# A hybrid decoder layer on one core: gate weights loaded once per group from GpSimd's queue, the low half of the recurrent y stored from another buffer, a split wait in the gate unit, and the chunk locals moved behind the head numerator

## The reference

```python
u = rmsnorm(h, pre_mix_gain)
proj = u @ w_in                      # rg_x, rg_gate, q, k, v, o (512 columns each), i, f (4 each)
# recurrent half (8 blocks of 64 channels)
xc = causal_conv4(rg_x)
r = sigmoid(xc @ gate_r_w + gate_r_b);  i = sigmoid(xc @ gate_i_w + gate_i_b)   # block diagonal
a = exp(-8 * r * softplus(-lam));  b = sqrt(1 - a*a) * (i * xc)
h_rg = scan(h = a*h + b);  y_rg = rmsnorm(h_rg * gelu(rg_gate))
# mLSTM half (4 heads of 128, chunkwise)
q, k = silu(causal_conv4(q)), silu(causal_conv4(k))
log_i, log_f = i + b_i, log_sigmoid(f + b_f)
# per chunk: cumulative log_f, running maxima, p = exp(d - m), scores = (q k^T) * p
# num = scores v + w * q C_prev ; state C carried from chunk to chunk
y_ml = headrmsnorm(sigmoid(o) * num / max(|den|, exp(-m)))
h = h + rmsnorm(concat(y_rg, y_ml) @ w_out)
h = h + rmsnorm(relu(rmsnorm(h) @ w_up)**2 @ w_down)
```

## Time and profile before

| | |
|---|---|
| median of 3 runs | 2432.08 us (2430.23 to 2432.1) |
| span of the profiled execution | 2429.1 us |
| TensorE busy | 2306.5 us, 95% of the span |
| VectorE busy | 1288.3 us, 53% |
| ScalarE busy | 659.1 us, 27% |
| GpSimd busy | 800.2 us, 33% |
| DMA, 16 engines | 244.82 MB, mean 101 GB/s |

### The profile page before, as it was taken

One profiled execution on the slowest core, in us unless ns is written; L12 is line 12 of the kernel. 1 busy time (PEld: TensorE's weight loads), 2 busy tenths in 40 slices (PEclk: granted clock), 3 DMA queues, 4 the chain that ended last, 5 costly groups with the idle time before them and its releaser, 6 DMA issues.

```text
span 2429.1 us, 29582 instructions
## 1 busy us (share of the span) xinstructions
PE 2306.5 (95%) x10549; PEld 1896.2 (78%) x10549; DVE 1288.3 (53%) x1665; ACT 659.1 (27%) x1187; POOL 800.2 (33%) x490
## 2 busy tenths in 40 slices
PE   5988899999996899999999999979899999999998
PEld 4766688888885687888888888868688888888886
DVE  4666556666656365534534543527745534534535
ACT  5554345445445231101100110124201101100112
POOL 6000000000000137534733743520845634733630
PEclk9999899999998899999999999989899999999999
DMA  5335454545432642111101211247311111211203
GB/s 192 115 132 201 150 163 148 189 131 181 159 113 70 220 144 79 52 35 52 60 28 50 69 35 37 101 141 249 120 44 61 52 34 52 69 35 35 69 17 147
DMA packets 123944, 244.82 MB, mean 101 GB/s; under 512 B 13040, under 2 KB 46160, under 8 KB 123888
## 3 DMA queue, kind: packets, MB, share of 16 engines
q1 hardware_dynamic: 95280, 141.20, 17.4%
q0 software_dynamic: 26304, 94.52, 12.3%
q10 hardware_dynamic: 2304, 8.39, 0.9%
HBM read 193.61 MB, written 50.46 MB: 100 GB/s over the span
## 4 chain that ended last, share of the span: by engine, by line
PE 61%; DVE 3%; ACT 1%; issue 1%; DMA 1%; POOL 0%; ACTq 0%; DVEq 0%; SPq 0%; PEldq 0%; POOLq 0%
PE o_ps L1373 20%; PE o_ps L1374 20%; PE o_ps L1375 20%; DVE o_relu L1649 1%; ACT o_ps L1474 1%; DVE o_ff_lo L1653 1%; PE o_ps L1397 0%; DMA o_v_lo<-ylo_d 0%; DVE o_acc L1593 0%; DVE o_v_lo L1642 0%; DMA o_w_raw<-in_w_out 0%; DVE o_h_t L1609 0%; ACT o_ff_hi L1531 0%; DVE o_h_t L1622 0%; POOL w_lo L1344 0%
## 5 line engine op out<-in xcount | busy, mean ns | idle before, releaser
L1342 POOL TENSOR_TENSOR w_hi<-o_w_raw,one 128x1024 fp32r<-128x1024 f32 x100 | 191.5, 1915 | 683.7 <-PE o_ps L1375 589.8
L1373 PE MATMUL o_ps<-o_v_hi,w_hi 128*128 128x512 f32 x1024 | 400.1, 391 | 4.8 <-DVE o_v_lo L1642 4.8
L1374 PE MATMUL o_ps<-o_v_lo,w_hi 128*128 128x512 f32 x1024 | 399.6, 390 | 0.0
L1375 PE MATMUL o_ps<-o_v_hi,w_lo 128*128 128x512 f32 x1024 | 399.6, 390 | 0.0
L1663 DVE TENSOR_TENSOR o_acc<-o_ps,o_acc 128x512 f32<-128x512 f32 x224 | 154.1, 690 | 377.1 <-PE o_ps L1375 376.6
L1649 DVE TENSOR_TENSOR o_relu<-o_relu 128x512 f32<-128x512 f32 x128 | 221.0, 1727 | 180.9 <-ACT o_relu L1528 180.3
L1528 ACT ACTIVATE o_relu<-o_ps 128x512 f32<-128x512 f32 x128 | 76.5, 598 | 872.1 <-PE o_ps L1375 842.9
L436 PE MATMUL m_unit_ps<-u_hi,w_hi 128*128 128x512 f32 x768 | 310.0, 404 | 0.0
L436 PE MATMUL m_unit_ps<-u_hi,w_lo 128*128 128x512 f32 x768 | 301.2, 392 | 0.0
L436 PE MATMUL m_unit_ps<-u_lo,w_hi 128*128 128x512 f32 x768 | 300.3, 391 | 0.0
L1653 DVE TENSOR_TENSOR o_ff_lo<-o_relu,o_ff_hi 128x512 fp32r<-128x512 f32 x128 | 243.6, 1903 | 90.7 <-ACT o_ff_hi L1531 90.7
(11 more groups left out here) (281 smaller groups left out, 3443.8 us busy)
## 6 DMA issues: line engine op xcount, KB each, us to landing
o_w_raw<-in_mlp_w_up POOLq DMA_DIRECT2D x64, 512.0 KB, 4.6
o_w_raw<-in_mlp_w_down POOLq DMA_DIRECT2D x64, 512.0 KB, 3.6
u_hi<-uhi_d SPq DMA_DIRECT2D x12, 2048.0 KB, 10.8
u_lo<-ulo_d SPq DMA_DIRECT2D x12, 2048.0 KB, 15.2
w_raw<-in_w_in POOLq DMA_DIRECT2D x24, 512.0 KB, 5.7
m_rows<-rows_d SPq DMA_DIRECT2D x16, 512.0 KB, 5.3
o_v_hi<-yhi_d SPq DMA_DIRECT2D x16, 512.0 KB, 5.5
o_v_lo<-ylo_d SPq DMA_DIRECT2D x16, 512.0 KB, 6.4
```

What stands on the lines that cost most here:

```text
L1342: pool.tensor_tensor(w_hi[i], w_raw[i % 2][:], one_bc, ALU.mult).then_inc(w_split[i], 1)
L1373: nc.tensor.matmul(dst, sh, mh, start=(i == 0), stop=False)
L1374: nc.tensor.matmul(dst, sh, ml, start=False, stop=False)
L1375: last = nc.tensor.matmul(dst, sl, mh, start=False, stop=(i == n - 1))
```

## The change

Five edits, all in `build_mixers`:

1. The gate weights of a group are loaded once, from GpSimd's queue (`load_gate_w`), instead of once a step from SP's. Group 0's four transfers stand between the loads of x tile 1 and `gate_rows(0)`; those of groups 1 to 3 behind the last raw weight of the group, with a wait for the last gate product of the group before. SP's `load_rows` no longer waits for `gate_mm`. TensorE waits for 64 more counts a group, not a step.
2. The low part of the recurrent y is written to `b_t` and stored from there. ScalarE's square of g_x waits only for VectorE's subtraction of the step before; the wait for the stores' landing moves to the square that writes `b_t`.
3. The gate unit waits for tiles 0 to 5 of u_lo, and in front of tile 6's matmuls for all eight.
4. `chunk_locals` moves on VectorE from behind `states` to behind `head_numerator`.
5. The semaphore `gate_w_in` is created outside the mixers' own set.

```diff
@@ load_rows (SP)
                 for n in ("iw", "s_old", "parg0", "kw_arg"):
                     sp.wait_ge(s[n], s.freed(p))
-                sp.wait_ge(s["gate_mm"], s.freed(p))
                 if isinstance(p, int) and p < NT:
                     sp.wait_ge(rows_out, 32 * (p + 1))
-                for r, name in enumerate(("rg_gate_r_w", "rg_gate_i_w")):
-                    for h in range(2):
-                        sp.dma_start(gate_w[64 * h:64 * h + 64, r, 64 * h:64 * h + 64],
-                                     a[name][0].rearrange("(g h) i j -> h i g j", h=2)[h, :, ds(p // NT, 1), :]
-                                     ).then_inc(gate_w_in, 16)
                 sp.dma_start(rows[:], k["rows_d"][:, ds(p * TILE, TILE)].partition_broadcast(P)
                              ).then_inc(rows_in, 16)
@@ store_rg (SP)
-                sp.dma_start(k["ylo_cols"][:, ds(m * TILE, TILE)], g_y[:].bitcast(F32)).then_inc(yrg_out, 16)
+                sp.dma_start(k["ylo_cols"][:, ds(m * TILE, TILE)], b_t[:]).then_inc(yrg_out, 16)
@@ GpSimd
+            def load_gate_w(g):
+                if not isinstance(g, int) or g:
+                    pool.wait_ge(s["gate_mm"], s.ready(g * NT - 1))
+                for r, name in enumerate(("rg_gate_r_w", "rg_gate_i_w")):
+                    for h in range(2):
+                        pool.dma_start(gate_w[64 * h:64 * h + 64, r, 64 * h:64 * h + 64],
+                                       a[name][0].rearrange("(g h) i j -> h i g j", h=2)[h, :, ds(g, 1), :]
+                                       ).then_inc(gate_w_in, 16)
-            for t in range(NT - 1):
+            load_x(1)
+            load_gate_w(0)
+            gate_rows(0)
+            for t in range(1, NT - 1):
                 load_x(t + 1)
                 gate_rows(t)
...
                     load_raw((c + 3) % 6, g + c // 3)
+                load_gate_w(g)
...
+            load_gate_w(NG - 1)
@@ gates_and_transposes, gate_unit (TensorE)
-                pe.wait_ge(gate_w_in, m * 64 + 64)
+                pe.wait_ge(gate_w_in, (m // NT) * 64 + 64)
...
-                pe.wait_ge(ulo_made, KT * (p + 1))
+                pe.wait_ge(ulo_made, KT * p + gap_tiles[5][0])
                 if p:
                     pe.wait_ge(prev_made, p)
                 for c in range(KT):
+                    if c == gap_tiles[5][0]:
+                        pe.wait_ge(ulo_made, KT * (p + 1))
@@ ScalarE: sigmoids_1, exponentials
-                act.wait_ge(yrg_out, m * 32 + 32)
+                freed("yrg_lo", m)
                 nc.scalar.activation(g_y[:], g_x[:], ACT.Square).then_inc(s["g2"], 1)
...
+                act.wait_ge(yrg_out, m * 32 + 32)
                 nc.scalar.activation(b_t[:], a_t[:], ACT.Square).then_inc(s["a2"], 1)
@@ VectorE: rg_low, period
-                nc.vector.tensor_tensor(g_y[:].bitcast(F32R), g_y[:], yrg_hi[:].bitcast(F32), ALU.subtract
+                freed("h", m + 1)
+                nc.vector.tensor_tensor(b_t[:].bitcast(F32R), g_y[:], yrg_hi[:].bitcast(F32), ALU.subtract
...
-                if gates:
-                    chunk_locals(p)
                 if mix:
                     recurrence(m)
                 low_of("k")
                 if mix:
                     head_numerator(m)
+                if gates:
+                    chunk_locals(p)
                 low_of("v")
```

More of the change, by code:

```diff
@@ L187, in build_mixers @@
         w_split = {u: sem("w_split_" + u) for u in UNITS}
-        gate_w_in = sem("gate_w_in")
+        gate_w_in = k["gate_w_in"]
         raw_first = k["raw_in_p"]
@@ L1759, in hybrid_layer @@
             "gates_in": ctx.enter_context(nc.semaphore("gates_in")),
+            "gate_w_in": ctx.enter_context(nc.semaphore("gate_w_in")),
         }
```

## The result

The change takes 2399.16 us (median of 4 runs, 2398.41 to 2401.31) where the kernel before takes 2432.09 (2430.23 to 2432.93) beside it: a ratio of 0.9873, 95% interval 0.986 to 0.9885, so 33 us or 1.3% faster. The forecast was 2401 us in a range of 2396 to 2410, with 31.6 us of gain in the span; the spans differ by 2429.1 - 2396.6 = 32.5.

What follows compares the result with a forecast made beforehand. TensorE, busy for 95% of the 2429.1 us span, bounds the kernel; gain is possible only where it waits. 14.8 + 5.4 + 8.95 + 9.7 less 7.3 gives 31.6 us: span 2397.5, forecast 2401 us, range 2396 to 2410.

Steps and rivals of the forecast that it cites:

- Edit 1, 14.8 us: At the gate products in periods 1 to 4, TensorE's waits for gate weights go: 14.8 us, nothing in their place.
- GpSimd's issues: Four issues ahead of gate_rows(0) in period 0 cost 0, at most 2.1 us; the skill's port rule would add 2.8.
- Edit 2, 0 us as cover: ScalarE's square stops waiting for DRAM, so its gate unit copy comes earlier; cover for the gate products, 0 us gain.
- Edit 3, 5.4 us: At the gate unit, TensorE's waits for the last low part of u go: 5.4 us.
- Edit 4, 8.95 us less 7.3: At the square sums, den2's waits go (8.95 us); new waits of 1.9, 1.9 and 3.5 us in periods 1 to 3.
- The clock, 9.7 us: TensorE's clock losses behind four removed waits in the early periods go: 1.7, 3.4, 1.7 and 2.9 us, together 9.7.
- no new loss: Behind the new TensorE waits of 0.7 to 2.1 us, no new clock loss was counted.
- if the clock still falls between 120 and 280 us: Sign that the prediction is wrong: TensorE's clock was to be 1.00 from period 1 to 300 us.
- rival A: The clock falls behind the new waits too, once in each of periods 1 to 3: 5.1 us, 2406; chance 0.18.
- B: Period 4's wait only changes name: TensorE waits 3.7 us for m_y_t plus 1.7 of clock, 2406; chance 0.07.
- C: No change: VectorE bounds the early periods throughout, and 27 of the 31.6 us return; chance 0.03.
- D: Slower: ScalarE stands for b_t's stores in every step from landings of 16.7 us; 2453 us at 21; chance 0.03.

Runs made afterwards that it cites:

- e7: The change with VectorE's convolution of x later and its split of q moved into an earlier pause: 2396.42 us (0.9856).
- e8: The change with GpSimd's four issues of gate weights behind gate_rows(0) instead of ahead of it: 2401.38 us (0.9876).
- e3: The change with the low y made in g_y again, ScalarE's square waiting until it has landed in DRAM: 2408.31 us (0.991).
- e2: The change with the gate unit waiting for all eight low parts of u again: 2406.65 us (0.9907).
- e5: The kernel before with only the chunk locals moved behind the head numerator: 2426.60 us (0.9984).
- e9: The change run once more, unaltered, beside another kernel on the same chip: 2399.24 us (0.9873).
- e1: The change with the chunk locals back ahead of the recurrence: 2406.51 us (0.9905).
- e4: The kernel before with only the gate weights loaded once per group, issued by GpSimd: 2411.52 us (0.9921).

## Why the prediction was right

**Edit 1, 14.8 us.** All four waits went, also the 9.22 us of period 4, with nothing in their place. The reason given holds in the trace. VectorE and, in the second row, ScalarE at the end of period 3:

```profile
239.05 0.73 DVE L992 SCALAR_TENSOR_TENSOR m_y_t<-m_s_ps,par,m_yml_hi 128x512 fp32r<-128x512 f32 x1
```

```profile
233.74 0.62 ACT L739 ACTIVATE m_yrg_hi<-m_g_y 128x512 fp32r<-128x512 f32 x1
```

m_y_t ends at 239.78, and TensorE is due at the transposes of o at 238.84 + 1.72 = 240.56. The margin is 0.8 us; the prediction had 1.1 (256.7 against 257.8). e7 used it up, and a wait of 0.85 us stood exactly there.

**GpSimd's issues.** All sixteen issues of gate weights, in ns min/median/max:

```profile
L345 POOL DMA_DIRECT2D m_gate_w<-in_rg_gate_r_w x8: 531/538/718, 42.5 to 568.5; - x8
L345 POOL DMA_DIRECT2D m_gate_w<-in_rg_gate_i_w x8: 522/529/562, 43.5 to 569.6; - x8
```

One of them took 0.18 us over the median, in the pair from 405.06 us, beside VectorE instructions of 0.55 us and more. e8, which takes the first four out of the way, is no faster. Of the rule of the Trainium skill ("SBUF — State Buffer", section "SBUF: two separate sides"), by which the prediction would have added 2.8 us, the four issues of period 0 say nothing. VectorE, the third value, did no work beside them:

```profile
42.48:44.57 2.09, 2.09 (x11) 1.70 (x11) 0.00 (x0) 0.00 (x0) 2.09 (x6) 1.00 0.90 310
```

So the 2.8 us could not come here, whatever the rule; the prediction's reason (the longest issue is 0.07 us over the shortest) was not what decided it.

**Edit 2, 0 us as cover.** Right as cover, and e3 gives it its price: 9.1 us.

**Edit 3, 5.4 us.** Right in waits (5.3 in e2).

**Edit 4, 8.95 us less 7.3.** The den2 waits are exact. The new waits were 1.6 in periods 1 and 2 for 1.9, and in period 3 1.63 + 0.24 for 1.4 + 2.1. The last term is the one that was mis-sized as a wait, though not in its effect: e8, whose clock stayed up until then, has both near what the prediction put (1.63 and 1.82):

```profile
232.87 0.33 PE L519 MATMUL m_s_ps<-ident,m_y_tok 128*128 128x128 f32 x1 [1.82 <-DVE m_y_tok L870]
```

**The clock, 9.7 us.** The four losses of the earlier trace rows went, but "no new loss" and "clock 1.00 up to 300 us" were wrong in one place. By the prediction's own sign ("if the clock still falls between 120 and 280 us") this step failed, and the sum held all the same. From the wait for the locals to the head transposes, the change and then e8:

```profile
224.78:232.50 7.72, 7.48 (x26) 5.67 (x26) 6.83 (x20) 0.40 (x2) 0.88 (x1) 0.78 0.22 69
```

```profile
225.15:232.87 7.72, 5.90 (x26) 4.50 (x27) 6.83 (x20) 1.20 (x3) 0.88 (x1) 1.00 0.22 69
```

The same code, the same wait of 1.63 us ahead, the same 7.72 us in between, since VectorE's y_tok ends the stretch in both. In the change the clock is 0.78 over it, a loss of 1.7 us, and the wait for y_tok shrinks from 1.82 to 0.24. The loss was taken out of a wait that stood behind it anyway, and so it was free. In e8 the clock fell behind the second wait instead:

```profile
232.87:239.00 6.13, 6.13 (x23) 4.82 (x24) 5.92 (x13) 4.49 (x7) 1.50 (x2) 0.72 0.54 166
```

There 6.13 x 0.28 = 1.7 us were paid in full, and interval 3-4 is 47.10 against 45.49. That is rival A, in one of three periods. Six kernels have both of these waits in period 3. In five of them (the change, e2, e3, e5 and e9) the clock is 0.78 over the 7.7 us behind the first and the second is 0.2 to 0.3 us; only e8 fell behind the second. The section "HAM oscillation — how this bites in real kernels" of the Trainium skill ("TensorE: Matmul & The Clock Gate") describes the cost as one that returns with each burst of matmuls; in these traces the pattern is there, but a fall cost 1.7 us or nothing, by what TensorE waited for next.

The sum of 9.7 us is also less firm than it looks. Where the prediction says that "the trace agrees for four of the waits and not for the one of 2.38", it overlooks a line of the earlier trace rows: behind the wait of 2.34 us at 150.39 the clock is 1.00 too. Of the 9.7 us, 5.1 stood behind den2's three waits, and waits of the same length lost 1.7, 0 and 3.4 us in the kernel before, 3.4, 1.7 and 1.7 in e1, and 0, 3.4 and 3.2 in e4. That the change gained just this sum holds for the execution of the kernel before that was profiled.

**The remaining 0.9 us** between 31.6 and 32.5 is the first line of the balance, 1.5 us more than forecast (in period 0 the clock was 1.00 here, after a wait for v_t of 0.58 us; before it was 0.84 over the 9.6 us behind a wait of 2.43, 1.5 us that the prediction's sum does not have), and the last, 1.0 us less. Over the experiments v_t's wait ran from 0.31 to 4.1 us, and between the change (0.58), e9 (0.81, the same code) and e1 (3.64, other code only behind that point). That is startup, and luck.

**Rivals.** B and C did not come. The wait that B names came with e7, when the margin was gone, and not for B's reason (ScalarE's yrg_hi late). D, the store of b_t: line 266's landings in the change are

```profile
DMA to landing us min/median/max: 2.2/2.3/10.3
```

so the longest of 16 was 10.3 us, against the 16.7 from which ScalarE would stand.

## What to carry to other kernels

Count a balance by intervals between points that every step passes, and give every removed wait the next late thing behind it with its margin in us: that margin (1.1 us here) says how much the next edit can gain before the wait only changes its name. An edit that "gains nothing" by itself can be what lets the others gain, so test it by taking it out of the whole (9.1 us here). When an engine becomes early, look at what stands in front of the late operand in its producer's program order; three pure reorderings of VectorE's work gave another 4.6 us. Count a removed wait's clock as a range and not as a figure: behind waits of 2.4 us it was 0 to 3.4 us here.

## What the runs showed that was not expected

- A fall of TensorE's clock ahead of a wait for another engine costs nothing: 0.78 over 7.72 us in the change, and interval 3-4 is 1.6 us shorter than in e8 with 1.00 over the same stretch.
- Which of two waits of 1.6 and 1.8 us the clock falls behind differs between kernels whose first wait is the same to 0.01 us: behind the first in five, behind the second in one.
- Behind the same wait for den2 (2.36 to 2.38 us) the clock was 1.00 over 7.7 us in some periods and 0.54 or 0.55 over as long a stretch in others, 0 or 3.4 us (e1, e4 and the kernel before).
- The same store of 256 KB landed in 2.3 us (median) and in 10.3 where it was issued right behind loads of x; e3 turned that into 8.70 us of a standing ScalarE.
- One wait in the output part is 8.3 or 10.9 us in two executions of the same kernel, which sets the floor for comparing single profiles: 2.6 us.
